# The first unit behind four norms runs on an operand without the inverse root

## The reference

```python
y = xf * lax.rsqrt(jnp.mean(xf * xf, axis=-1, keepdims=True) + EPS)   # rms_norm, times gain g
return x * (1 + scale[:, None, :]) + shift[:, None, :]                # modulate
a = h @ w_up                                                          # the first product behind it
```

## Time and profile before

| | us |
|---|---|
| median of 3 runs | 1732.64 (1732.54 to 1736.28) |
| span of the profiled execution, first to last instruction | 1730.9 |
| PE busy | 1658.9 |
| DVE busy | 1302.2 |
| ACT busy | 819.2 |
| POOL busy | 243.0 |

### The profile page before, as it was taken

How to read it: one execution, slowest core, us unless ns; L and a number is a source line. 1 busy time by engine, 2 the same in 40 slices (tenths; PEclk the granted TensorE clock), 3 DMA queues, 4 the chain that set the end, 5 groups by cost and what they waited for, 6 DMA issues and landing times.

```text
span 1730.9 us, 28129 instructions
## 1 busy us (share of the span) xinstructions
PE 1658.9 (96%) x11542; PEld 1464.1 (85%) x11542; DVE 1302.2 (75%) x1818; ACT 819.2 (47%) x1186; POOL 243.0 (14%) x199
## 2 busy tenths in 40 slices
PE   6999989999999999999999999969999999899999
PEld 3887768788788777986999999959999999699887
DVE  5687863887988878857578777797988868758574
ACT  3433752543133323646554546575635444555352
POOL 0423001011001111540310121013000220030000
PEclk8999999999999999999999999989999999999999
DMA  8644002243565458320347566635998966137552
GB/s 345 254 150 167 2 26 73 98 146 116 192 240 219 178 193 307 122 74 1 122 158 277 196 218 239 212 123 172 358 365 321 342 219 223 46 125 277 183 173 95
DMA packets 46575, 317.83 MB, mean 184 GB/s; under 512 B 5232, under 2 KB 6256, under 8 KB 12272
## 3 DMA queue, kind: packets, MB, share of 16 engines
q1 hardware_dynamic: 45936, 312.68, 50.0%
q0 software_dynamic: 512, 3.35, 0.5%
HBM read 314.96 MB, written 1.05 MB: 183 GB/s over the span
## 4 chain that ended last, share of the span: by engine, by line
PE 80%; DVE 11%; ACT 3%; issue 3%; POOL 2%; DMA 1%; SPq 0%; DVEq 0%; ACTq 0%
PE PM L1679 20%; PE PM L1680 19%; PE PM L1681 19%; PE PM L1833 5%; PE PM L1835 3%; PE PM L1963 2%; DVE wlo L1054 2%; PE PX L1999 1%; DVE acc L1088 1%; PE PX L1872 1%; PE PO L2025 1%; PE PX L1652 1%; DMA raw<-in_ada 1%; PE PO L2014 1%; PE PX L1929 1%
## 5 line engine op out<-in xcount | busy, mean ns | idle before, releaser
L1054 DVE TENSOR_TENSOR wlo<-raw,whi 128x2048 fp32r<-128x2048 f32 (+2 forms) x199 | 437.8, 2200 | 73.1 <-ACT whi L733 72.6
L1679 PE MATMUL PM<-H,whi 128*128 128x256 f32 (+1 forms) x1526 | 480.2, 315 | 7.7 <-DVE H L1480 3.0
L1680 PE MATMUL PM<-H,whi 128*128 128x256 f32 (+1 forms) x1526 | 476.2, 312 | 0.0
L1681 PE MATMUL PM<-H,wlo 128*128 128x256 f32 (+1 forms) x1526 | 476.1, 312 | 0.0
L733 ACT ACTIVATE whi<-raw 128x2048 fp32r<-128x2048 f32 (+3 forms) x204 | 365.5, 1792 | 143.2 <-PE PM L1681 48.7
L1679 PEld LDWEIGHTS PM<-H,whi 128*128 128x128 f32 x1526 | 291.1, 191 | 32.1 <-issue 7.9
L1681 PEld LDWEIGHTS PM<-H,wlo 128*128 128x128 f32 x1526 | 291.1, 191 | 16.5
L1680 PEld LDWEIGHTS PM<-H,whi 128*128 128x128 f32 x1526 | 291.3, 191 | 15.9
L1088 DVE SCALAR_TENSOR_TENSOR acc<-raw,silc,acc 128x512 f32<-128x512 f32 x328 | 245.1, 806 | 5.3 <-DMA raw<-in_ada 4.2
L1679 PE MATMUL PM<-G,whi 128*128 128x256 f32 (+1 forms) x608 | 192.7, 317 | 1.7 <-DVE X L1238 1.6
L1680 PE MATMUL PM<-G,whi 128*128 128x256 f32 (+1 forms) x608 | 190.8, 314 | 0.0
(11 more groups left out here) (243 smaller groups left out, 2675.4 us busy)
## 6 DMA issues: line engine op xcount, KB each, us to landing
raw<-in_ada SPq DMA_DIRECT2D x104, 1024.0 KB, 5.2
raw<-in_wm SPq DMA_DIRECT2D x93, 1024.0 KB, 5.1
raw<-in_wl SPq DMA_DIRECT2D x68, 1024.0 KB, 5.1
raw<-in_wl SPq DMA_DIRECT2D x32, 704.0 KB, 4.3
raw<-in_wm SPq DMA_DIRECT2D x5, 768.0 KB, 4.5
raw<-in_wm SPq DMA_DIRECT2D x4, 704.0 KB, 4.1
X<-in_x SPq DMA_DIRECT2D x1, 2048.0 KB, 12.2
bias<-in_bias POOLq DMA_DIRECT2D x1, 2048.0 KB, 11.0
```

The costliest lines, as they stand in the source:

```text
L1054: dve.tensor_tensor(wslot(wlo, i, usize(u)), slot_raw(n, usize(u)), wslot(whi, i, usize(u)).bitcast(F32), ALU.subtract)\
L1679: pe.matmul(out, st_hi, mv_hi, start=first, stop=False)
L1680: pe.matmul(out, st_hi, mv_lo, start=False, stop=False)
L1681: return pe.matmul(out, st_lo, mv_hi, start=False, stop=last)
```

## The change

For norms 3, 4, 5 and 8 the first unit behind the norm (`PLAIN`) multiplies X m, without root and shift. The split operand `Phi`, `Plo` has 258 columns per chunk: 256 tokens, and the shift s (high part and remainder likewise) in two more, so that column 256 of the result is W s. ACT and DVE form it chunk by chunk while the feeding units still run (`plain_hi`, `plain_lo`), the last one or two chunks at the norm. PE runs the unit with the sums and the spread between its steps (`unit_plain`) and without the warming matmuls, which are gone for these norms. The normalised H is formed as before, but the second unit is now the first to use it. After the fifth remainder DVE repairs the first unit's result in PSUM (`fix`): times r, plus W s. ACT reads it out when that is done and all eight pieces are. The third unit's weight split stands on ACT behind the second piece, and POOL takes the remainder of it too.

```diff
-WARM_NORM = {1: 2, 2: 2, 3: 2, 4: 2, 5: 2, 6: 2, 8: 2}
-WARM_SPREAD = {1: 3, 2: 2, 3: 2, 4: 2, 5: 2, 6: 3, 8: 2}
-WARM_SUM = {4: 2, 5: 2, 6: 2}
+WARM_NORM = {1: 2, 2: 2, 6: 2}
+WARM_SPREAD = {1: 3, 2: 2, 6: 3}
+WARM_SUM = {6: 2}
...
+PLAIN = {3: ("up", "L1"), 4: ("lin", "M0"), 5: ("w1", "M0"), 8: ("w1", "M1")}
+PW = 258
...
+def plain_chunks(u):
+
+    n = fed_norm(u)
+    before = UNITS[u["i"] - 1]
+    return chunks_of(before) if n in PLAIN and fed_norm(before) == n else []
...
+POOL_SPLIT += [first_of(*key) + 2 for key in PLAIN.values()]
...
+            def plain_hi(n, chunks):
+
+                v = norm_vec(n)
+                for k in chunks:
+                    if k == 0:
...
+                        act.activation(plain_shift(Phi), shift_of(n), ACT.Copy).then_inc(*tick("phi", (n, "shift")))
+                    act.wait_ge(*at("xres", (n, k)))
+                    act.activation(plain(Phi, k), X[:, k * 512:k * 512 + 256], ACT.Identity, scale=modc(v + 1, 0, k))\
+                        .then_inc(*tick("phi", (n, k)))
...
+            def summed(u):
+
+                if plain_norm(u):
+                    act.wait_ge(*at("hlo", last_piece(plain_norm(u))))
+                return at("fixed", u["i"]) if plain_norm(u) else at("unit", u["i"])
...
                 n = fed_norm(u)
                 if n is not None:
+                    if plain_chunks(u):
+                        plain_hi(n, plain_chunks(u))
...
                     _, n, st, W = step
+                    if n in PLAIN:
+                        plain_hi(n, chunks_of(fed_units(n)[-1]))
                     if n not in (0, 7):
                         root(n, W)
...
+                        if n in PLAIN and s == 1:
+                            split_hi(first_of(*PLAIN[n]) + 2)
...
-                    if (u["kind"], u["idx"]) != ("lpart", 0):
+                    if (u["kind"], u["idx"]) != ("lpart", 0) and not plain_norm(u):
                         split_hi(i + 2)
...
+            def fix(u, n):
+
+                i = u["i"]
+                dve.tensor_copy(rinvs[:, :], PO[:, 0:256]).then_inc(*C.link("dve_chain"))
+                dve.wait_ge(*at("unit", i))
+                both = view(pm(i, 0, 1024), "p (c t) -> p c t", c=2)
+                link(dve.tensor_copy(bcol[:, 0:2], both[:, :, 256]))
+                dve.tensor_tensor(both[:, :, 0:256], both[:, :, 0:256], rinvs[:, :].unsqueeze(1).to_broadcast([P, 2, 256]), ALU.mult)\
+                    .then_inc(*C.link("dve_chain"))
+                dve.wait_ge(*C.last)
+                for c in range(2):
+                    ins = dve.tensor_scalar(pm(i, c * 512, 256), pm(i, c * 512, 256), bcol[:, c:c + 1], None, ALU.add)
+                ins.then_inc(*tick("fixed", i))
...
                             ins.then_inc(*tick("hlo", (n, s - 1)))
+                        if n in PLAIN and s == 5:
+                            fix(UNITS[first_of(*PLAIN[n])], n)
...
+            def unit_plain(u, n):
+
+                i, kt = u["i"], u["kt"]
+                pe.wait_ge(*at("plo", (n, "shift")))
+                for k in range(kt):
+                    pe.wait_ge(*at("plo", (n, k)))
+                    for c in range(2):
+                        w0 = k * u["cols"] + c * 128
+                        ins = three(pm(i, c * 512, PW), wslot(whi, i, 128, w0), wslot(wlo, i, 128, w0),
+                                    Phi[:, k * PW:k * PW + PW], Plo[:, k * PW:k * PW + PW], k == 0, k == kt - 1)
+                    if k == 0:
+                        sumsq(*late[0])
+                    elif k == 1:
+                        for a in late[1:]:
+                            sumsq(*a)
+                    elif k == 3:
+                        spread(n, u["T"])
+                ins.then_inc(*tick("unit", i))
```

More of the change, by code:

```diff
@@ L228, in chunks_of, with plain_norm, fed_units @@
     return [u["idx"] % KD]
+def plain_norm(u):
+    return next((n for n, (kind, st) in PLAIN.items() if u["kind"] == kind and u["st"] == st and u["idx"] == 0), None)
+def fed_units(n):
+    return [u for u in UNITS if fed_norm(u) == n]
+def plain_chunks(u):
+    n = fed_norm(u)
+    before = UNITS[u["i"] - 1]
+    return chunks_of(before) if n in PLAIN and fed_norm(before) == n else []
 def ada_plan():
@@ L420, in build @@
         nsink = sb("nsink", 16)
+        bcol = sb("bcol", 8)
+        rinvs = sb("rinvs", 256)
+        Phi, Plo = (G2[:, a:a + KD * PW] for a in (NL * 256, HALF * 512 + NL * 256))
         assert cursor[0] <= 229344, cursor[0]
@@ L552, in wide, with plain, plain_shift, shift_of @@
             return u["st"] == "M1" and (u["kind"] == "w2" or u["kind"] == "w1" and u["i"] >= LAST_ADA + 2)
+        def plain(buf, k):
+            return buf[:, k * PW:k * PW + 256]
+        def plain_shift(buf):
+            return view(buf, "p (k c) -> p k c", c=PW)[:, :, 256:258]
+        def shift_of(n):
+            v = norm_vec(n)
+            return mod[:, v * 16:v * 16 + 8].unsqueeze(2).to_broadcast([P, KD, 2])
+        def norm_vec(n):
+            return vec_base({0: "L0", 1: "L0", 2: "L1", 3: "L1", 4: "M0", 5: "M0", 6: "KV", 7: "M1", 8: "M1"}[n]) + (3 if n in (1, 3, 5, 8) else 0)
         def ff_part(k, low):
@@ L820, in evac @@
                     l, j = int(u["st"][1]), u["idx"]
-                    act.wait_ge(*at("unit", i))
+                    act.wait_ge(*summed(u))
                     for part in range(2):
@@ L1247, in residual, with plain_lo @@
                             dve.wait_ge(*at("pm_dve", i))
+            def plain_lo(n, chunks):
+                v = norm_vec(n)
+                for k in chunks:
+                    if k == 0:
+                        dve.wait_ge(*at("phi", (n, "shift")))
+                        dve.tensor_tensor(plain_shift(Plo), shift_of(n), plain_shift(Phi).bitcast(F32), ALU.subtract)\
+                            .then_inc(*tick("plo", (n, "shift")))
+                    dve.wait_ge(*at("phi", (n, k)))
+                    dve.scalar_tensor_tensor(out=plain(Plo, k), in0=X[:, k * 512:k * 512 + 256], scalar=modc(v + 1, 0, k),
+                                             in1=plain(Phi, k).bitcast(F32), op0=ALU.mult, op1=ALU.subtract).then_inc(*tick("plo", (n, k)))
+            def fix(u, n):
[10 more added lines that the diff above has]
+                ins.then_inc(*tick("fixed", i))
             def evac(u):
@@ L1528, in _ @@
                     v = vec_base(st) + (3 if n in (1, 3, 5, 8) else 0)
+                    if n in PLAIN:
+                        plain_lo(n, chunks_of(fed_units(n)[-1]))
                     if n not in (0, 7):
@@ L1618, in _ @@
                         split_lo(i + 2)
+                    if plain_chunks(u):
+                        plain_lo(fed_norm(u), plain_chunks(u))
                     for v in turned_at(i):
@@ L1799, in unit @@
                     unit_in_step(u, n)
+                    return
+                n = plain_norm(u)
+                if n:
+                    unit_plain(u, n)
                     return
@@ L2074, in _ @@
             for step in PROGRAM:
+                if step[0] == "norm" and step[1] in PLAIN:
+                    continue
                 if step[0] in ("norm", "attn"):
@@ L2097, in _ @@
                     unit(u)
-                    for a in late:
-                        sumsq(*a)
+                    if not plain_norm(u):
+                        for a in late:
+                            sumsq(*a)
                     late = []
```

8 lines of the change are left out of this document (7 added, 1 removed).

## The result

The changed kernel takes 1767.5 us (median; 1767.02 to 1768.77, 4 runs) against 1734.18 before in the same job (1732.54 to 1736.28, 4 runs): ratio 1.0194, 95% interval 1.0181 to 1.0207. The forecast was 1736.0 with a range of 1728 to 1742, so the loss is about ten times the forecast one. The profiled execution took 1767.43 us, its span is 1765.6, 34.7 above that of before.

A forecast was written before the change was run, and what follows sets the result against it. PE, busy 96%, was taken as the bound, with DVE's chain making it wait at the norms. Norms 3, 4, 5 and 8: 1.3 + 3.5 - 0.45 - 1.2 = +3.2 us; 1732.64 + 3.2 = 1736 us, range 1728 to 1742.

The forecast's parts named there:

- The step that failed first: Third unit's weight remainder on POOL: done 8 us after the first product, in time; frees DVE of 2.29 us.
- I take 0 on the path; without that cover 0.4 to 0.8 us: Making the plain operand on ACT and DVE before each norm: mostly in idle time, so 0 us on the path.
- The repair: Five DVE instructions behind the fifth remainder at each norm: 2.13 us, bounded by 1.3 and 3.
- The terms of the order: Norms 3, 4, 5, 8: +1.3, +3.5, -0.45, -1.2 us, repair and norm 4's clock loss included.
- DVE is nearly full here: Norm 5: fourth unit's weights ready only at 1215.2, PE at 1214.4, so the gain there is just 0.45 us.
- The clock: Third lin unit behind norm 4: starts with 3.4 us at 1.2 GHz, half of it lost, 1.7 us.
- rival 2: Clock falls already in the second unit's 2.1 us stall, in all four norms: +5.7 us, 1738.3 us; chance 0.20.
- Rival 4: Matmuls of 258 columns run at another rate; at half rate 23 us more, 1759 us; chance 0.02.
- The table load behind norm 4: ACT behind norm 4: load 1.28 us without the skill's drain of about 1.38, which would make norm 4 1.4 us later.

The follow-up runs named there:

- split_after_plain: The changed kernel with the third unit's weight remainder on DVE and GpSimd's split of the second unit waiting for the plain operand: 1748.41 us, ratio 1.0089.
- order_free: split_after_plain without the plain remainders, the repair and GpSimd's wait for the plain operand: 1736.96 us, ratio 1.0015 to the kernel before.
- warm_in_stalls: split_after_plain with warm matmuls added in PE's two waits at each norm: 1750.07 us, ratio 1.0079 to the kernel before.
- before_early_pool: The kernel before with only the third unit's early split on ACT and its remainder on POOL: 1759.14 us, ratio 1.0147.

## Why the prediction was wrong

The account by ratios, each step one experiment apart: GpSimd's split of the third unit 15.4 us (1.0194 to 1.0105), its hold on the plain remainders, as far as a later split removes it, 2.8 (to 1.0089), the repair 8.3 (to 1.0041), the remainders 5.4 (to 1.0010), the new order itself 1.7. Sum 33.6, by construction. The 2.8 and the 1.7 are not clear of noise, the other three are.

- **The step that failed first** reads: "POOL takes the remainder of these weights (4.51 us in its like the earlier trace rows) and is done 8 us after the first product, in time; DVE is freed of 2.29 us, but only behind its chain". It was in time for PE and took 4.4 us from DVE, in the middle of the chain whose every 0.4 us I had counted. I asked when the instruction would be done, and not what its engine shares with the one I had just called the bound. This alone puts the result outside the range.
- **"I take 0 on the path; without that cover 0.4 to 0.8 us"** for the plain operand failed too. "six of the eight pairs fall into idle time of the feeding units" priced them at 0.48; beside GpSimd's square additions they take 0.96 each (rows under split_after_plain), and the last ones over 4 us together. It cost 5.4 to 6.1 us by the experiments that leave the remainders out, besides the hold.
- **The repair** was right in place and size: 2.13 forecast; 2.05 us from 860.52 to 862.57 measured, 8.3 for four against 8.5.
- **The terms of the order** hold less. Without the repair, and without the 1.7 us for the clock, they say -0.8, -0.3, -2.6 and -3.3 at the four norms; order_free's third units start 0.5, 0.0, 1.7 and 1.8 us earlier, and in its time nothing is left of that. I had allowed for this giving back in norm 5 alone ("DVE is nearly full here"). What is behind it is shown in part: in norm 4 the slow clock (1.57 us), in norm 5 the wait of 2.06 us at 1231.27. In that profiled execution PE's clock also fell in the attention stage behind (mean 0.83 from 1471 to 1491, 1.00 in before), in code that no variant changes; eight other variants show a fall there, six variants, the changed kernel and the one before don't. What starts it stays open. It may belong to the execution and not to the kernel: the 21 runs of the kernel before in that job lie between 1730.66 us (mean clock 0.987) and 1738.77 (0.984).
- **The clock** fell as forecast behind norm 4 (0.50 from 1076 to 1082), and also in the second unit of norm 3 (0.50 from 860 to 864), as rival 2 had it, though behind the hold's wait of 3.44 us and not that of the repair. In the second unit it costs nothing, as PE waits for DVE ahead of the third one anyway: in warm_in_stalls the clock stays up, and the third unit of norm 3 starts 19.74 us behind the norm's start, 19.72 in split_after_plain. In the third unit of norm 4 it is paid, as forecast: 1.57 us in order_free against 1.7 charged; the same stretch takes 57.64 us in the changed kernel (55.10 before) at a mean of 0.95. With the clock kept up by warm_in_stalls only 0.70 us comes back there, as PE then waits for DVE.
- **Rival 4** (another rate at 258 columns) is out: 0.12 us from start to start. The table load behind norm 4 took 1.28 us with the first activation 0.02 behind it (1074.24, 1075.54), as in before; the drain that the Trainium skill ("ScalarE: Activation LUTs", What ACT_TABLE_LOAD costs) adds to each switch isn't in these rows.
- **What would have given it away**: the square additions above. With "a GpSimd instruction of 4.5 us holds an H remainder" the sum would have been 3.2 + 15.7 = 19 us, and with the remainders held at the spread (1.0 + 1.5 + 1.2 + 1.0 us) 23.6. That is 1756 us, still below 1767: the rest is the remainders' own load and gains that didn't come.

## What to carry to other kernels

Before work moves to an engine "with time to spare", look in the trace for an instruction of that engine whose duration changes beside one of the bound engine; then place it only where the bound engine reads PSUM or waits. Where one engine's queue sets the distance from a norm to the next free bank, neither a new order of PE nor a later place in that queue helped in these runs; work taken out of it did. And price an instruction put into "idle time" by a row of its kind beside its new neighbours. When an instruction makes PE wait longer, look at the granted clock behind the wait too: it costs where PE is then the engine that the others wait for.

## What the runs showed of the hardware that I had not expected

- A DVE instruction with two SBUF inputs stands still until a GpSimd tensor_tensor that runs is done (4.40 us against 0.48), and a GpSimd one behind a DVE split as well (1.49 against 0.79). A DVE instruction with one input in PSUM doesn't (0.44 beside a running one).
- On one weight tile of 128x2048 GpSimd needs 4.5 us where DVE needs 2.28, so what it takes off DVE it can take back twice.
- A DVE multiply of 128x512 that reads and writes PSUM takes 0.70 us, a like one from and to SBUF 0.69.
- A wait of PE can cost more than its length: behind waits of 3.4 to 3.7 us the granted clock was at 1.2 GHz, and where PE had no other wait this took another 1.57 us (order_free, norm 4) or 1.2 to 2.4 us a norm (before_early_pool). Where PE waited for DVE anyway it took nothing.
